# First attention of a transformer layer on Trainium2: two softmax maps added on GpSimd before one turn by the identity

## The reference, cut to what matters

```python
def diff_attention(q, k, v, lam):          # per block of 128 query rows
    s = jnp.einsum('bhmqd,bhmkd->bhmqk', qi, k).astype(jnp.float32) * scale
    s = jnp.where(kpos[None, :] <= qpos[:, None], s, -jnp.inf)
    p = jax.nn.softmax(s, axis=-1)
    pd = p[:, :, 0] - lam * p[:, :, 1]
    return jnp.einsum('bhqk,bhkd->bhqd', pd.astype(v.dtype), v)

def memory_attention(q, mem_n, w_kv, qnorm, knorm):
    ...
    p = jax.nn.softmax(s, axis=-1)
    return jnp.einsum('bhsm,bmhd->bshd', p.astype(v.dtype), v).reshape(Bz, S, M_WIDTH)
```

## Time and profile before

| what | value |
|---|---|
| median of 3 runs | 3061.44 us (3060.88 to 3066.49) |
| the profiled execution's own time | 3061.13 us |
| its span | 3059.3 us |
| busy share of the span | PE 92%, PEld 53%, DVE 38%, ACT 22%, POOL 10% |
| granted TensorE clock, mean | 0.962 of full speed |
| the stage of the change | 319 to 431 us of the span |

### The profile page before, as it was taken

The page is one execution under the profiler, slowest core; times in us unless marked ns, Lnnn a source line. Parts: engine busy times, 40 slices in busy tenths (PEclk is TensorE's granted clock), DMA queues, the critical chain, the costliest instruction groups (busy, mean ns, idle before and its releaser), DMA issues. The chain is left out here.

```text
span 3059.3 us, 42583 instructions
## 1 busy us (share of the span) xinstructions
PE 2822.5 (92%) x18114; PEld 1633.1 (53%) x18114; DVE 1152.4 (38%) x2254; ACT 664.6 (22%) x1525; POOL 295.4 (10%) x383
## 2 busy tenths in 40 slices
PE   8999998999898899999999797999999699989988
PEld 3344663446576445558888643664444444444443
DVE  1051451195345178626656466440013211111111
ACT  3110331111233164314333115331001000000000
POOL 0000110000001000006666201000000000000000
PEclk9999998997888999999999899999999799999999
DMA  5451014241001420101101313005120499999998
GB/s 200 174 206 55 1 50 110 69 83 57 0 1 35 163 84 34 40 23 32 31 31 37 108 68 131 1 1 228 66 71 37 195 427 427 426 427 426 427 426 358
DMA packets 129843, 441.23 MB, mean 144 GB/s; under 512 B 21446, under 2 KB 34890, under 8 KB 102129
## 3 DMA queue, kind: packets, MB, share of 16 engines
q1 hardware_dynamic: 129654, 438.50, 37.2%
HBM read 428.21 MB, written 10.26 MB: 143 GB/s over the span
## 5 line engine op out<-in xcount | busy, mean ns | idle before, releaser
L357 PE MATMUL banks<-weight_ring,rows_turned 128*128 128x512 f32 (+1 forms) x1576 | 670.7, 585 | 18.3 <-DMA weight_ring<-in_w_in 14.4
L357 PEld LDWEIGHTS banks<-weight_ring,rows_turned 128*128 128x128 f32 x1576 | 295.2, 192 | 382.8 <-issue 378.7
L2536 PE MATMUL banks<-rows_turned,weight_ring 128*128 128x512 f32 (+1 forms) x640 | 225.6, 512 | 1.5 <-PEq L1404 1.5
L4072 PE MATMUL banks<-weight_ring,chosen_turned 128*64 128x512 f32 (+1 forms) x696 | 174.5, 558 | 10.2 <-DMA weight_ring<-in_w_up 6.5
L4072 PE MATMUL banks<-expert_weights_early,chosen_turned 128*64 128x512 f32 (+1 forms) x672 | 169.3, 558 | 11.6 <-DMA expert_weights_early<-in_w_up 8.0
L2536 PEld LDWEIGHTS banks<-rows_turned,weight_ring 128*128 128x128 f32 x640 | 122.5, 192 | 96.1 <-issue 86.9
L1472 PE MATMUL banks<-weight_ring,mix_turned 128*128 128x512 f32 x320 | 138.3, 593 | 3.0 <-DMA weight_ring<-in_l_w_out 1.6
L4174 DVE TENSOR_TENSOR hidden<-hidden,banks 128x512 f32<-128x512 f32 (+1 forms) x24 | 14.0, 639 | 325.5 <-PE banks L4072 325.5
L4072 PEld LDWEIGHTS banks<-weight_ring,chosen_turned 128*64 128x64 f32 x696 | 62.4, 137 | 97.7 <-issue 93.9
L357 PE MATMUL banks<-weight_ring,branch_turned 128*128 128x512 f32 x256 | 112.3, 593 | 0.8 <-ACT branch_turned L3469 0.8
L4072 PEld LDWEIGHTS banks<-expert_weights_early,chosen_turned 128*64 128x64 f32 x672 | 60.8, 137 | 95.2 <-issue 91.4
(11 more groups left out here) (551 smaller groups left out, 4438.4 us busy)
## 6 DMA issues: line engine op xcount, KB each, us to landing
weight_ring<-in_w_gate SPq DMA_DIRECT2D x29, 1408.0 KB, 17.2
weight_ring<-in_w_up SPq DMA_DIRECT2D x29, 1408.0 KB, 15.2
expert_weights_early<-in_w_gate SPq DMA_DIRECT2D x28, 1408.0 KB, 18.9
expert_weights_early<-in_w_up SPq DMA_DIRECT2D x28, 1408.0 KB, 16.4
expert_weights_early<-in_w_down SPq DMA_DIRECT2D x36, 1024.0 KB, 17.0
weight_ring<-in_w_down SPq DMA_DIRECT2D x35, 1024.0 KB, 17.5
weight_ring<-in_l_w_in SPq DMA_DIRECT2D x15, 2048.0 KB, 8.9
weight_ring<-in_ada_w SPq DMA_DIRECT2D x12, 2048.0 KB, 8.1
```

Source lines behind the costliest of these rows:

```text
L357: ins = kit.nc.tensor.matmul(self.bank(u), lhsT, rhs, start=(k == 0), stop=(k == nk - 1))
L2536: ins = nc.tensor.matmul(kit.ps[:, bank(u), 0:n], w[:, k, f * P:(f + 1) * P], hT[:, k, h0:h0 + n], start=(k == 0), stop=(k == KD - 1))
L4072: ins = nc.tensor.matmul(kit.ps[64 * s:64 * s + 64, 3 * mat + i, 0:nn], xe[:, p % 2, k0 + j, s * CAP:(s + 1) * CAP], w[s][:, j, n0:n0 + nn ...
```

## The change

For a causal unit the second map is no longer weighed on the way through PE. DVE makes one ratio per row, minus lambda times the first sum over the second; POOL multiplies the second map's probabilities by it in place and adds them to the first map's. PE then turns the sum alone, by products with the identity. The weight of the row, one over the first sum, is kept in `row_weights` and applied by the group's `finish`. Memory units have no POOL work any more: PE turns their maps with the identity right after the exponentials, and their `finish` first multiplies by the weights and then by the gate. `probs` has four buffers instead of three, and turn, copy, sum and finish each come one iteration later.

```diff
-        probs = kit.sb(st, "probs", [P, 3, 2, 512])
+        probs = kit.sb(st, "probs", [P, 4, 2, 512])
...
             def turn_probs(u):
-                pe.wait_ge(weighted.sem, weighted(u + 1))
+                merged = units[u]["merged"]
+                if merged:
+                    pe.wait_ge(weighted.sem, weighted(merged_until[u + 1]))
+                else:
+                    pe.wait_ge(exp_ready.sem, exp_ready(u + 1))
...
                 for a in range(0, units[u]["n"], P):
-                    for m in range(2):
-                        out = kit.ps[:, 4 + (u % 2 if merged else m), a:a + P]
-                        ins = nc.tensor.matmul(out, probs[:, u % 3, m, a:a + P], diagonal[:, u % 3, m, :], start=(m == 0 or not merged), stop=(m == 1 or not merged))
+                    for m in range(1 if merged else 2):
+                        ins = nc.tensor.matmul(kit.ps[:, 4 + (u % 2 if merged else m), a:a + P], probs[:, u % 4, m, a:a + P], kit.ident, start=True, stop=True)
...
-            for i in range(U + 3):
+            for i in range(U + 4):
                 if i < U:
                     scores(i)
-                if 2 <= i <= U + 1:
-                    turn_probs(i - 2)
-                if i >= 3:
-                    sum_values(i - 3)
+                if 3 <= i <= U + 2:
+                    turn_probs(i - 3)
+                if i >= 4:
+                    sum_values(i - 4)
...
             def weigh(u):
                 dve.wait_ge(exp_ready.sem, exp_ready(u + 1))
-                step(dve, nc.vector.reciprocal(inv[:, u % 4, :], sums[:, u % 4, :]))
-                factor = units[u]["factor"]
...
+                if units[u]["merged"]:
+                    step(dve, nc.vector.reciprocal(inv[:, u % 4, :], sums[:, u % 4, :]))
+                    nc.vector.tensor_copy(by_row, inv[:, u % 4, 0:1])
+                    nc.vector.scalar_tensor_tensor(ratio[:, u % 4:u % 4 + 1], sums[:, u % 4, 0:1], units[u]["factor"], inv[:, u % 4, 1:2], ALU.mult, ALU.mult).then_inc(weights_ready.sem, 1)
                 else:
...
+                    step(dve, nc.vector.reciprocal(row_weights[:, units[u]["group"], at:at + 2], sums[:, u % 4, :]))
...
-                if 2 <= i <= U + 1:
-                    keep_first(i - 2)
-                if i >= 4 and last_of[units[i - 4]["group"]] == i - 4:
-                    finish(units[i - 4]["group"])
+                if 3 <= i <= U + 2:
+                    keep_first(i - 3)
+                if i >= 5 and last_of[units[i - 5]["group"]] == i - 5:
+                    finish(units[i - 5]["group"])
...
-                    if i >= 3:
-                        act.wait_ge(turned.sem, turned(i - 2))
+                    if i >= 4:
+                        act.wait_ge(turned.sem, turned(i - 3))
...
-                if i >= 2 and 1 in parts(i - 2):
-                    u = i - 2
+                if i >= 3 and 1 in parts(i - 3):
+                    u = i - 3
...
         def gpsimd(pool):
             for u in range(U):
-                pool.wait_ge(weights_ready.sem, weights_ready(u + 1))
-                if u >= 3:
-                    pool.wait_ge(turned.sem, turned(u - 2))
-                nc.gpsimd.tensor_tensor(diagonal[:, u % 3, :, :], kit.ident.unsqueeze(1).broadcast_to([P, 2, P]),
-                                        weights[:, u % 4, :].unsqueeze(2).broadcast_to([P, 2, P]), ALU.mult).then_inc(weighted.sem, 1)
+                if units[u]["merged"]:
+                    n = units[u]["n"]
+                    first, second = probs[:, u % 4, 0, 0:n], probs[:, u % 4, 1, 0:n]
+                    pool.wait_ge(weights_ready.sem, weights_ready(merged_until[u + 1]))
+                    kit.pool_step(pool, nc.gpsimd.tensor_tensor(second, second, ratio[:, u % 4:u % 4 + 1].broadcast_to([P, n]), ALU.mult))
+                    nc.gpsimd.tensor_tensor(first, first, second, ALU.add).then_inc(weighted.sem, 1)
...
+        def weighted_heads(dst, psum, w):
+            H = w.shape[1]
+            return nc.vector.tensor_tensor(heads(dst, 64), heads(psum, 64), w.unsqueeze(2).broadcast_to([P, H, 64]), ALU.mult)
...
-            finishes.append(lambda dve, psum, t=t: nc.vector.tensor_copy(y[:, t, V:V + 512], psum))
+            finishes.append(lambda dve, psum, w, t=t: weighted_heads(y[:, t, V:V + 512], psum, w))
...
+            step(dve, weighted_heads(dst, psum[:, 0:256], w[:, 0:4]))
+            return nc.vector.tensor_tensor(dst, dst, y[:, t, MG:MG + 256], ALU.mult)
```

More of the change, by code:

```diff
@@ L925, in attend_joined @@
         exp_ready = kit.counter("exp_ready", U)
-        weights_ready = kit.counter("weights_ready", U)
-        weighted = kit.counter("probs_weighted", U)
+        merged_until = [sum(x["merged"] for x in units[:u]) for u in range(U + 1)]
+        weights_ready = kit.counter("weights_ready", merged_until[U])
+        weighted = kit.counter("probs_weighted", merged_until[U])
         turned = kit.counter("probs_turned", U)
@@ L1003, in weigh @@
                 dve.wait_ge(exp_ready.sem, exp_ready(u + 1))
[L1004 to L1010 removed]
+                at = units[u]["weights_at"]
+                by_row = row_weights[:, units[u]["group"], at:at + 1]
+                if units[u]["merged"]:
+                    step(dve, nc.vector.reciprocal(inv[:, u % 4, :], sums[:, u % 4, :]))
+                    nc.vector.tensor_copy(by_row, inv[:, u % 4, 0:1])
+                    nc.vector.scalar_tensor_tensor(ratio[:, u % 4:u % 4 + 1], sums[:, u % 4, 0:1], units[u]["factor"], inv[:, u % 4, 1:2], ALU.mult, ALU.mult).then_inc(weights_ready.sem, 1)
+                else:
+                    step(dve, nc.vector.reciprocal(row_weights[:, units[u]["group"], at:at + 2], sums[:, u % 4, :]))
             def keep_first(u):
@@ L1022, in finish @@
                 dve.wait_ge(summed.sem, summed(last_of[g] + 1))
-                finishes[g](dve, values_bank(g)).then_inc(finished.sem, 1)
-            for i in range(U + 4):
+                finishes[g](dve, values_bank(g), row_weights[:, g, :]).then_inc(finished.sem, 1)
+            for i in range(U + 5):
                 if i < U:
@@ L1358, in memory_joined @@
             values = [[mem_v[:, m, 256 + h * 64:256 + (h + 1) * 64] for m in range(TM)] for h in (2 * f, 2 * f + 1)]
-            units.append(dict(maps=maps, n=MEM, causal=False, merged=False, values=values, at=(128 * f, 128 * f + 64), group=group0 + t, factor=None))
+            units.append(dict(maps=maps, n=MEM, causal=False, merged=False, values=values, at=(128 * f, 128 * f + 64), group=group0 + t, weights_at=2 * f))
     return units
@@ L1891, in first_layer, with finish_memory @@
                 values = [y[:, s, BV + h * 64:BV + (h + 1) * 64] for s in range(t + 1)]
-                units.append(dict(maps=maps, n=(t + 1) * P, causal=True, merged=True, values=[values], at=[64 * h], group=group, factor=signs[:, :]))
-            finishes.append(lambda dve, psum, t=t: nc.vector.tensor_copy(y[:, t, V:V + 512], psum))
+                units.append(dict(maps=maps, n=(t + 1) * P, causal=True, merged=True, values=[values], at=[64 * h], group=group, weights_at=h, factor=signs[:, 1:2]))
+            finishes.append(lambda dve, psum, w, t=t: weighted_heads(y[:, t, V:V + 512], psum, w))
         units += memory_joined(mqT, mkT, mem_kv, TX)
+        def finish_memory(dve, psum, w, t):
+            dst = y[:, t, AG:AG + 256]
+            step(dve, weighted_heads(dst, psum[:, 0:256], w[:, 0:4]))
+            return nc.vector.tensor_tensor(dst, dst, y[:, t, MG:MG + 256], ALU.mult)
         for t in range(TX):
-            finishes.append(lambda dve, psum, t=t: nc.vector.tensor_tensor(y[:, t, AG:AG + 256], psum[:, 0:256], y[:, t, MG:MG + 256], ALU.mult))
+            finishes.append(lambda dve, psum, w, t=t: finish_memory(dve, psum, w, t))
         attend_joined(kit, units, finishes)
```

9 lines of the change are left out of this document (4 added, 5 removed).

## The result

| | before | changed |
|---|---|---|
| median of 5 runs, us | 3061.44 (3058.45 to 3066.49) | 3098.90 (3063.85 to 3099.51) |
| profiled execution, us | 3061.13 (span 3059.3) | 3063.85 (span 3062.1) |
| the stage (first scores to SP's first issue behind it), us | 319.13 to 431.28: 112.1 | 318.90 to 436.57: 117.7 |

The ratio to before is 1.0095, 95% interval [1.0056, 1.0135]: slower by about 1%, where 3046.4 was forecast. The five runs are not one group: the profiled one took 3063.85 at a mean granted clock of 0.955, the other four 3096.42 to 3099.51 at 0.940 to 0.942.

A forecast was written before the change was run, and what follows sets the result against it. PE was taken to bound the kernel (busy 92% of the span), and after the change the wait for ACT's copy. Gains of 7.4, 4.4, 1.9 and 1.8, less 0.45, made 15.0 us: 3061.44 to 3046.4, range 3041 to 3054.

The forecast's parts named there:

- Ends of the stage: Stage start and drain: one more score pair at the lower clock offsets the halved first turn; 0, bounds -2 and +2.
- The prediction's own sign for this: Listed mark of a wrong forecast, in the changed stage: PE's clock under 1.00 past 330 us.
- Slower: PE's clock falls: Rival: clock falls in the 128-key group and stays down through memory attention; 26.9 us more, 3073; chance 0.05.
- Its deciding point: The clock rival holds if PE idles in one piece for something like 3.25 us; idle expected 0.23 an iteration.
- The sum: Whole stage: gains of 7.4, 4.4, 1.9 and 1.8 by key group, memory 0, less 0.45: 15.0 us.
- the second finish: End of memory attention: finish becomes two operations instead of one; 0.45 us more, bounds 0.4 to 0.9.
- POOL: Product and addition per causal unit: 1.04 and 1.27 us with 512 keys, 0.88 together with 128; close, not binding.
- DVE and POOL at once: DVE's last small weighting operation could wait for POOL; in the even case they don't meet, nothing charged.
- The loop through ACT's copy: PE's sum waits for ACT's copy behind the exponentials: periods at least 2.96, 2.45, 1.93, 1.42 us by key group.
- PE alone binds: Rival: the copy loop doesn't bind because ACT gets ahead; gain 20.7 us, 3040.8; chance 0.09.
- The gain is lost behind the stage: Rival: what follows the stage eats the gain, or the identity product isn't a shorter turn; 3061; chance 0.04.

The follow-up runs named there:

- a1: The changed kernel run once more, unaltered, for a second profile: one execution, 3084.66 us, stage 143.7 us.
- a3: Changed kernel plus 13 spare identity products ahead of the third scores, where PE waits: median 3059.96 us, ratio 1.0016.
- c2: Changed kernel plus 13 spare products ahead of the third scores and ACT's copy put before the exponentials, no repeated turns: median 3054.00 us, ratio 0.9998.
- a2: Changed kernel with every product of a causal unit's turn made twice: median 3065.01 us, ratio 1.0000.
- c3: Changed kernel with ACT's copy first, turns of units 0 to 2 made twice, 128-key turns three times, no spare products: median 3051.27 us, ratio 0.9962.
- b3: Changed kernel with spare products (13, then 2), turns of units 0 to 2 twice, 128-key turns three times, ACT's copy first: 3044.19 us, ratio 0.9947.
- b2: Changed kernel with spare products (13, then 2), turns of units 0 to 2 twice, 128-key turns three times, ACT's order unaltered: 3050.70 us, ratio 0.9960.
- b1: Changed kernel with only the turns of the eight 512-key units made twice: median 3061.79 us, ratio 1.0002.
- b4: Changed kernel with the score products of each causal unit made twice, turns left short: median 3115.19 us, ratio 1.013.
- a4: Kernel before with only the greater depth (four map buffers, turn and sum one iteration later): median 3064.38 us, ratio 1.0007.
- c1: Changed kernel with only ACT's copy put ahead of the exponentials: median 3090.10 us, ratio 1.0045.

## Why the prediction was wrong

- **Ends of the stage** is the step that failed. It priced the lower clock behind the 3.25 us wait for one more pair of scores and a first turn, and took 0, bounds -2 and +2. That stood on an unspoken premise: that the clock would return where it did in before. There the window from 329.3 us, right behind the first turn of eight, is at 0.99. But the change halves that turn, and with four products in it the lower level held for 44 us (323 to 367) in one profile and for 122 (320 to 442) in the other. By the table the first two groups cost 32.5 - 22.3 = 10.2 and 27.9 - 21.1 = 6.8 over forecast, of 20.6 in the stage. The prediction's own sign for this, a clock under 1.00 past 330 us, is what the profile shows. The median lies 52.5 over the forecast; a1's stage, 46.6 over it, covers most of that, if those runs are of its kind.
- **Slower: PE's clock falls** named the right engine and sign, at 0.05, and the place of the smaller loss; the larger lies at the start of the stage. Its deciding point, an idle piece of something like 3.25, was wrong, so that the sign came right is in part luck. The clock fell behind idle times of 0.58 (changed), 0.57 (a3, 2.00 - 1.43 in its window) and 0.49 (c2). That these waits alone brought the fall is not shown: in a2 it held through one of 0.66. The cost, late units and memory, was 0.8 + 3.6 = 4.4 in the changed profile; the 26.9 given for it took the memory part at half clock to the end, where it returned to 1.00 at 418 us. The window read for 128 keys, 393 to 411, also holds 3.9 us of memory attention (from 407.11).
- **The sum** holds where the clock does. At 1.00 the groups of a3 took 21.3, 20.7 and 16.2 (the first without the slow start that the forecast's 22.3 keeps), and c3's and b3's memory part 24.7 (0.45 for the second finish made it 24.6). The periods of 2.45 and 1.94 are as worked out. The 512-key one of 2.96 had no clean stretch in the changed kernel; in a3 it is 336.79 - 333.81 = 2.98, without idle time of PE. So there PE's own work binds, priced 2.94, and not the copy: b2 and b3, without and with the copy first, both take 23.1.
- **POOL**: 1.04 and 1.26 with 512 keys, 0.40 and 0.45 with 128 (0.88 for both was forecast). **DVE and POOL at once**: 0.23 on average for the operation that might have been held; the two met once, at the uneven start, for some 0.5 (0.70 against 0.21 as a rule). **The loop through ACT's copy**: shown with 384 and 256 keys by b3, which removes it, and with 256 and 128 by its waits.
- **PE alone binds**: b3, whose order of ACT's work this rival needs and the change doesn't have, lies between it and the forecast, and nearer to the forecast: 3044.19 against 3040.8 and 3046.4. It also carries spare products, so it tests neither sum exactly.
- **The gain is lost behind the stage**: not so in the main; b3's stage and median gain the same 16.7. From profile to profile what lies behind the stage varies between 2623 and 2639 us, before's own 2628 among them, and single times shouldn't be compared more finely than that; to a tenth, the agreement is luck. Part of this too is the clock: b3's profiled execution had a mean of 0.957 against before's 0.962, with its stage at 1.00, and took 2637 behind the stage.

Still open is what in the halved iteration keeps TensorE at its lower level, and why one execution leaves it at 367 us and another not. Shown is that doubling the turns brings the clock up (a2, b1, c3), that doubling the scores doesn't in the execution profiled (b4), and that neither the depth (a4) nor ACT's order (c1) decides it.

## To carry to other kernels

Ahead of pricing work taken from TensorE, look where in the trace its granted clock falls, and which instructions bring it back: if the change thins out those, price the whole stage at half clock as a case with a real chance, not as a tail. Where a stage begins behind a wait, spare products in that wait, whose result is overwritten, can pay: a stage of 99.6 against 117.7 in a3's profile. But four of ten runs of a3 still took 3088 or more; only with some turns repeated as well were all runs faster than before's median (b2, b3, and c3 without spare products). A busy share of 100% says nothing of speed until the clock column stands beside it.

## What was not expected of the hardware

PE was busy for 116.00 of 116.00 us at a granted clock of 0.50 (b4), and for 91.00 of 91.00 in c1. The Trainium skill, TensorE: Matmul & The Clock Gate, in its Part 1 on the clock gate, says that the array runs at 1.2 GHz by default and that activity releases it to 2.4. The two levels agree with these rows, 0.50 and 1.00; but records that follow each other without a gap did not release it here, so that sentence read alone would lead one to expect a rise that didn't come.

The rise came in or right behind products of the maps with the identity or the values: in the turn at 327.07 (a2), 331.92 (a4), 332.09 (c3) and 441.72 (a1), and at the end of the value sum at 365.18 (changed). And one program has several times: 3064, 3085 and 3099 for the changed kernel, three clusters for a3, while those whose clock is held up by repeated turns (a2, b1, b2, b3) stay within some 18 us.
